# First four up-projection tiles taken from x times the second norm's gain, with the norm's factor and the shift applied to the result; ffn state and first up weights loaded behind the head loop

## What is computed

```
x = x + gate1 * mixed                       # mixed = concat(...) @ w_o, [520, 1024]
h2 = rms_norm(x, norm2_g) * (1.0 + scale2) + shift2
up, ffn_buf_new = causal_dwconv(h2 @ w_up, ffn_buf, ffn_conv_w, ffn_conv_b)   # 2 * 2816 columns
val, gt = jnp.split(up, 2, axis=-1)
x = x + gate2 * ((jax.nn.gelu(gt) * val) @ w_down)
```

## Time and profile before

| | us |
|---|---|
| median of 3 runs (lowest to highest) | 948.32 (946.69 to 949.16) |
| the profiled execution | 949.23 |
| its span, first to last instruction | 947.4 |
| granted TensorE clock, mean | 0.991 of full |

### The profile page before, as it was taken

One profiled execution on the slowest core, in us unless ns is written; L12 is line 12 of the kernel. 1 busy time (PEld: TensorE's weight loads), 2 busy tenths in 40 slices (PEclk: granted clock), 3 DMA queues, 4 the chain that ended last, 5 costly groups with the idle time before them and its releaser, 6 DMA issues.

```text
span 947.4 us, 20112 instructions
## 1 busy us (share of the span) xinstructions
PE 919.8 (97%) x7805; PEld 858.7 (91%) x7805; DVE 637.4 (67%) x1241; ACT 513.1 (54%) x1147; POOL 184.3 (19%) x163
## 2 busy tenths in 40 slices
PE   5899999999999999999999989999999999999998
PEld 3588876799999999999899979999999999999997
DVE  2893378488888888888863667777777777722321
ACT  2414845689889889898863354444444443311111
POOL 0032323333333324333330301100000001000000
PEclk9999999999999999999998999999999999999999
DMA  9996732300212203202130423333333331653202
GB/s 338 332 281 222 223 134 102 146 2 23 91 59 77 90 24 112 90 24 90 46 91 23 113 60 90 89 89 90 92 96 98 97 97 50 161 153 80 63 1 91
DMA packets 107897, 100.12 MB, mean 106 GB/s; under 512 B 7125, under 2 KB 96597, under 8 KB 105770
## 3 DMA queue, kind: packets, MB, share of 16 engines
q1 hardware_dynamic: 104030, 77.91, 28.1%
q0 software_dynamic: 3456, 20.97, 6.2%
q10 hardware_dynamic: 340, 0.27, 0.1%
HBM read 96.41 MB, written 2.94 MB: 105 GB/s over the span
## 4 chain that ended last, share of the span: by engine, by line
PE 88%; DVE 6%; ACT 2%; DMA 2%; issue 1%; SPq 0%; POOL 0%; DVEq 0%; ACTq 0%; POOLq 0%
PE ps L890 51%; PE ps L1286 20%; PE ps L885 6%; PE ps L1247 2%; PE ps L1183 2%; PE ps L923 2%; DMA RW<-w_ada 2%; PE ps L1062 1%; PE ps L896 1%; PE ps L1282 1%; DVE RB L1996 1%; PE ps L1209 1%; DVE input_low L1929 1%; DVE up_weights_low L2371 0%; DVE small L1970 0%
## 5 line engine op out<-in xcount | busy, mean ns | idle before, releaser
L890 PE MATMUL ps<-normed_high,up_weights_high 128*128 128x260 f32 x704 | 142.5, 284 | 2.5 <-DVE normed_low L2392 2.4
L890 PE MATMUL ps<-normed_high,up_weights_low 128*128 128x260 f32 x704 | 142.5, 284 | 0.0
L890 PE MATMUL ps<-normed_low,up_weights_high 128*128 128x260 f32 x704 | 142.1, 284 | 0.0
L1791 ACT ACTIVATE up_weights_high<-RW 128x1024 fp32r<-128x1024 f32 x44 | 46.6, 1061 | 128.0 <-PE ps L890 128.0
L836 POOL TENSOR_TENSOR latents_low<-RB,latents_high 128x512 fp32r<-128x512 f32 x64 | 82.7, 1292 | 165.7 <-ACT latents_high L1667 165.6
L1286 PE MATMUL ps<-key_weights_high,latents_high 128*128 128x260 f32 x512 | 113.3, 302 | 0.1
L890 PEld LDWEIGHTS ps<-normed_high,up_weights_high 128*128 128x128 f32 x704 | 108.9, 189 | 3.1 <-issue 2.2
L890 PEld LDWEIGHTS ps<-normed_high,up_weights_low 128*128 128x128 f32 x704 | 109.1, 189 | 0.0
L890 PEld LDWEIGHTS ps<-normed_low,up_weights_high 128*128 128x128 f32 x704 | 108.7, 189 | 0.0
L1286 PE MATMUL ps<-key_weights_high,latents_low 128*128 128x260 f32 x512 | 103.1, 283 | 0.0
L1286 PE MATMUL ps<-key_weights_low,latents_high 128*128 128x260 f32 x512 | 103.1, 283 | 0.0
(11 more groups left out here) (350 smaller groups left out, 2069.5 us busy)
## 6 DMA issues: line engine op xcount, KB each, us to landing
RW<-w_ada SPq DMA_DIRECT2D x24, 1024.0 KB, 7.0
RW<-w_up SPq DMA_DIRECT2D x44, 512.0 KB, 5.1
RW<-w_down SPq DMA_DIRECT2D x8, 1408.0 KB, 7.3
RW<-w_in SPq DMA_DIRECT2D x11, 512.0 KB, 6.4
RB<-w_o SPq DMA_DIRECT2D x8, 512.0 KB, 4.2
RB<-x_prompt SPq DMA_DIRECT2D x2, 1024.0 KB, 12.2
o_y_p<-RB SPq DMA_DIRECT2D x4, 448.0 KB
cst<-consts SPq DMA_DIRECT2D x1, 844.5 KB, 12.0
```

The source lines that it names most:

```text
L890: last = mm(ps[j % 4][rows[0]:rows[1], h, 0:H], lhsT, src[:, h * H:(h + 1) * H], start=start, stop=stop)
L1791: A(wuH[:, KT * g:KT * g + KT, :], wup[:, c, KT * g:KT * g + KT, :], ACT.Copy).then_inc(s_whi, 1)
```

## The change

For the first four up tiles (lap 0) the kernel uses that the factor rstd is one number for each token. It multiplies x by gain = (1 + scale2) x norm2_g only (`x_high`, `x_low`), takes the product with the up weights, multiplies the result by `rs` (`first_scaled`, DVE) and adds the product of the shift as a bias (`first_evacuate`, ACT, and a small addition for the samples). For the shift's product the nine shift columns, and three more to fill, stand behind the 520 tokens: 532 columns, two halves of 266. The normed x (`hH`, `hL`) is still made, for laps 1 to 10, by the same two steps (the samples' columns now within them).

The order of each engine is rewritten around that. SP: state and first up weights are loaded before w_o tile 5. PE: the state's turns before output tile 6; no fillers; the norm's two sums inside the first up tile. ACT: Square and gained copy of x before `out_high`; up weights at k = 2; the state's copy at k = 5. DVE: gain and shift parts before the residuals; gained low parts and the samples' steps within them; the up weights' low parts at m = 3; then first_scaled 0, low part 3, the rest of `scaled`, first_scaled 1, and the eight `normed_low` between the second low part and the GELU wait of `mlp(0, 0)`. Slots: state and norm sum move to slot 3, the up tiles start in slot 1.

Cut to its core (addresses, semaphore names and the renumbering of jobs are left out):

```diff
@@ SP @@
             for m in range(KT):
+                if m == 5:
+                    bfull(sp, "pv", NS)
+                    sp.dma_start(fs_tok, t["state_ffn_conv"].rearrange("l b r (m c) -> (l r m) b c", c=P)).then_inc(s_fst, 16)
+                    for c in range(2):
+                        up_weights(c, bass.ds(P * c, P))
...
-            for m in range(2):
-                up_weights(m, bass.ds(P * m, P))
-            full(sp, J_WO[KT - 1])
-            sp.dma_start(fs_tok, t["state_ffn_conv"].rearrange("l b r (m c) -> (l r m) b c", c=P)).then_inc(s_fst, 16)
@@ PE @@
             for m in range(4, KT):
+                if m == 6:
+                    claim(pe, J_FST)
+                    pe.wait_ge(s_fst, 16)
+                    for b in range(NS):
+                        c = 512 * (b // 4) + 4 * FT * (b % 4)
+                        last = tr(flat(J_FST)[:, c:c + 4 * FT], fs_tok[:, b, :], 4 * FT)
+                    last.then_inc(psum_full[J_FST % 4], 1)
...
+            def first_products(e, g, k):
+
+                j = up_job(2 * e + g)
+                for n, (w, x) in enumerate(((wuH, x_high[k]), (wuH, x_low[k]), (wuL, x_high[k]))):
+                    for h in range(2):
+                        last = mm(ps[j % 4][:, h, 0:XH], w[:, KT * g + k, :], x[:, h * XH:(h + 1) * XH],
+                                  start=(k == 0 and n == 0), stop=(k == KT - 1 and n == 2))
...
+            for e in range(2):
+                for g in range(2):
+                    up_start(e, g, 0)
+                    for k in range(KT):
+                        if (e, g) == (0, 0):
+                            pe.wait_ge(s_xlo, k + 1)
+                            if k in (0, 4, KT - 1):
+                                pe.wait_ge(s_xs, 1 + (0, 4, KT - 1).index(k))
+                        last = first_products(e, g, k)
+                        if (e, g) == (1, 1) and k < KT - 1:
+                            last.then_inc(s_xused, 1)
+                        if (e, g, k) == (0, 0, 1):
+                            claim(pe, J_N2)
+                            pe.wait_ge(s_nsum, KT - 2)
+                            both(J_N2, ones, sq[:, 0, :], True, False)
+                        if (e, g, k) == (0, 0, 3):
+                            pe.wait_ge(s_sq, 2 * KT + 12)
+                            both(J_N2, ones, sq[:, KT - 1, :], False, True).then_inc(psum_full[J_N2 % 4], 1)
@@ ACT @@
             for k in range(KT):
+                act.wait_ge(s_x1, k + 1)
+                A(sq[:, k, :], xT[:, k, :], ACT.Square).then_inc(s_sq, 1)
+                A(x_high[k][:, 0:NP], xT[:, k, 0:NP], ACT.Identity, bias=small[:, 1:2], scale=gmod[:, k, 0:1]).then_inc(s_xhi, 1)
                 if k + 4 < KT:
                     out_high(k + 4)
-                act.wait_ge(s_x1, k + 1)
-                A(sq[:, k, :], xT[:, k, :], ACT.Square).then_inc(s_sq, 1)
-                if k == 3:
+                if k == 2:
                     bfull(act, "pv", NS)
                     up_high(0, 0, 1)
                     up_high(0, 1, 1)
...
+            def first_evacuate(n):
+
+                j = up_job(n)
+                act.wait_ge(s_first, n + 1)
+                A(UU[n // 2][:, n % 2, 2:2 + NP], scaled_up[:, 0:NP], ACT.Identity, bias=shifts_up[n % 2][:, 0:1]).then_inc(psum_free[j % 4], 1)
...
             up_high(1, 0, 1, up_job(0))
...
+            first_evacuate(0)
+            up_high(1, 1, 1, up_job(1))
+            first_evacuate(1)
+            up_high(0, 0, 2, up_job(2))
+            for k in range(KT):
+                normed_high(k)
+            first_evacuate(2)
+            act.wait_ge(s_cv, 1)
+            A(GE, CV[1], ACT.Gelu_apprx_tanh).then_inc(s_ge, 1)
+            up_high(0, 1, 2, up_job(3))
+            first_evacuate(3)
@@ DVE @@
             for m in range(KT):
                 residual(J_WO[m], m, 2 * KT, s_x1, m + 1)
                 if m + 4 < KT:
                     out_low(m + 4)
-                if m == 4:
+                if 0 < m < KT - 1:
+                    gained_low(m - 1)
+                if m == 3:
                     up_low(0, 0, 1)
                     up_low(0, 1, 2)
...
+                if m == 4:
+                    gained_samples(0, 4)
+                if m == 6:
+                    gained_samples(4, KT - 1)
+                    gained_low(KT - 2)
+            gained_samples(KT - 1, KT)
+            gained_low(KT - 1)
...
+            def scaled(k):
+
+                V.tensor_tensor(h2[:, k, NP:T], gsr[:, k, :], dshift[:, k, :], ADD)
+                V.scalar_tensor_tensor(h2[:, k, 0:NP], xT[:, k, 0:NP], gmod[:, k, 0:1], rs[:, 0:NP], MUL, MUL).then_inc(s_hp, 1)
...
+            def first_scaled(n):
+
+                j = up_job(n)
+                full(dve, j)
+                if n > 0:
+                    dve.wait_ge(psum_free[up_job(n - 1) % 4], free_value(up_job(n - 1)))
+                shift = shifts_up[n % 2]
+                st.did(V.tensor_copy(shift, ps[j % 4][:, 1, T - XH:T + 9 - XH]))
+                st.did(V.tensor_tensor(scaled_up[:, 0:XH], ps[j % 4][:, 0, 0:XH], rs[:, 0:XH], MUL))
+                st.seq(V.tensor_tensor(scaled_up[:, XH:T], ps[j % 4][:, 1, 0:T - XH], rs[:, XH:T], MUL))
+                V.tensor_tensor(UU[n // 2][:, n % 2, 2 + NP:2 + T], scaled_up[:, NP:T], shift[:, 1:9], ADD).then_inc(s_first, 1)
+
+            dve.wait_ge(s_rs, 7)
+            st.seq(V.tensor_tensor(gsr[:, :, :], gs[:, :, :], rs[:, NP:T].unsqueeze(1).to_broadcast([P, KT, NS]), MUL))
+            scaled(0)
+            scaled(1)
+            first_scaled(0)
+            up_low(1, 0, 3)
+            for k in range(2, KT):
+                scaled(k)
...
+            first_scaled(1)
+            mlp(0, 0, 2, normed_lows)
+            first_scaled(3)
+            mlp(0, 1, 2)
+            with dve.Fori(1, FT // 2 - 1) as i:
```

189 lines of the change are left out of this document (97 added, 92 removed).

## The result

| | before | after |
|---|---|---|
| median (lowest to highest), us | 948.32 (946.13 to 949.97), 20 runs | 950.24 (947.12 to 953.99), 20 runs |
| ratio after / before, 95% interval | | 1.0024 (1.0014 to 1.0034) |
| profiled execution, us | 949.23 | 948.87 |
| its span | 947.4 | 947.1 |
| granted clock, mean | 0.991 | 0.995 |

A forecast was written before the change was run, and what follows sets the result against it. PE bounds the kernel, with a 10.7 us hole waiting for the norm before the up projection. Items of 11.05 replace it (+0.3); clock 1.2 and POOL contention 1.0 make +2.5, so 950.8 us, range 945.0 to 955.5.

The forecast's parts named there:

- the clock term: After the sixth up tile's wait PE may restart at half clock: 1.2 us net, bounds 0 and 3.4.
- Items 1 and 3: Output projection: tile 4 waits 0.75 us for its low weights, tile 7 waits 1.1 for tile 4's slot.
- Item 2: The state's eight turns move into the output projection: 0.85 us, and 0.14 until slot 3 is evacuated.
- Item 4: The norm's two sums move inside the first up tile: 2.0 us, and 0.1 waiting for the last POOL addition.
- Contention: DVE and POOL operations slow each other where they fall together at 542 to 549: 1.0 us, bounds 0 and 2.5.
- Item 6: The sixth up tile waits 5.2 us for its low part: DVE's queue of 31.5 against PE's 26.4.
- Item 7: The seventh up tile waits 0.4 us: DVE's convolution and low part take 6.15 against PE's 5.77.
- Rival A: The forecast itself: the hole is traded for a wait at the sixth up tile; 947 to 952.5 us, chance 0.47.
- Rival B: Faster: DVE reaches the sixth low part in time by overlap or earlier GELU; 944.0 us, chance 0.16.
- Rival C: Slower: DVE and POOL exclude each other from 538 to 549, delaying slot and second sum; 953.8 us, chance 0.30.
- Rival D: First tiles' operands are late too, leaving a 3 to 4 us hole before the up projection; 954.3 us, chance 0.07.
- The hidden terms: Early loads, small gain and shift operations on DVE, and the state's copy on ACT stand in existing waits, costing nothing.

The follow-up runs named there:

- e4: The changed kernel with ACT's out_high(k + 4) ahead of Square and gained copy, and DVE's two first up low parts behind residual 4; 949.80 us, ratio 1.0028.
- e8: The changed kernel with POOL adding only 8 of 520 columns of the squares, so its norm is wrong (a probe); 950.32 us, ratio 1.0029.
- e1: The changed kernel with the first GELU issued ahead of first_evacuate(2) on ACT; 947.44 us, ratio 0.9998.
- e10: The changed kernel with the third up tile's low part made twice on DVE; 950.50 us, one run.
- e2: The changed kernel with ten filler matmuls between the fifth up tile and the wait for the sixth low part; 950.97 us, ratio 1.0040.
- e5: The changed kernel with the sixth up low part right behind normed_low, and ACT's sixth high part and GELU before the third tile's evacuation; 948.69 us, ratio 1.0011.
- e6: e5 with the seventh, eighth and ninth up low parts also moved earlier on DVE, ACT's high parts in the same order; 943.17 us, ratio 0.9948.
- e7: e6 with e4's two edits, and the norm's sums behind the fifth and seventh step of the first up tile; 941.74 us, ratio 0.9939.
- e3: The kernel before with only the early state and up-weight loads, turns before output tile 6, state's copy on ACT and after's slots; 949.29 us, ratio 1.0007.
- e9: e7 with the tenth and eleventh up low parts also moved earlier on DVE, ACT's high parts likewise; 942.23 us, ratio 0.9943, on another chip.
- e11: e6 with the third up tile's low part made twice on DVE; 946.45 us, one run.
- e12: The changed kernel again without any edit, on another chip; 951.28 us, ratio 1.0031.

## Why the prediction was right, point by point

The forecast of 950.8 was 0.6 over the median; D came out at +2.53 for +2.5. That is closer than its terms deserve. As prices its terms add up to 13.2 in place of the hole's 10.7, and D gives 13.2 too (10.7 + 2.53), but counted from start to start single terms are off by up to 0.3 either way, and the clock term agreed by luck.

- **Items 1 and 3, the stops at output tiles 4 and 7.** Forecast 0.75 and 1.1, seen 0.78 and 1.06 of idle time, released as foretold by the low weights and by residual 4's second half. Counted from the start of one product to the start of the next they cost 1.0 and 1.3, as the idle time counts from a modelled end. Their mechanism was right, but they could not be won back singly: e4 took both away, half of the gain went into a longer wait at the sum and the rest, and more, into the half clock behind that wait. The hole taken as a sum of PE's stops was right as bookkeeping and wrong as a list of what each stop is worth.
- **Item 2, the turns.** Forecast 0.85, seen 0.6 (531.23 to 531.81); the slot's 0.14 did not show.
- **Item 4, the sums inside the first tile.** I gave each pair 1.0 and the wait 0.1. The pairs took 0.76 and 0.68 (547.26 to the product of 548.02, 549.70 to 550.38), the wait 0.86. The sentence that PE would pass the first tile without a stop was wrong in this step: I had looked at the low parts of x and at the last Square, and left out that DVE's rows ahead of it would be stretched (1.1 at 539.92, 0.26 at 544.27), which I had priced only as a lump in another place. DVE came to residual 7 at 547.59, which is 550.5 on the scale of before (the first residual stands 2.92 later there), where I had 548.9.
- **Contention, 1.0 (bounds 0 and 2.5).** Measured by e8: 1.13 at the sixth tile, with the additions' own length in it. The wait of 0.86 is its visible part, so item 4 and contention together were forecast at 3.1 and came to 2.3 (0.86, 0.76 and 0.68), or 2.8 with the slower first products behind each.
- **Item 5, 266 columns.** Forecast 0.5, measured 0.75: three such tiles take 17.87 (552.81 to 570.68), 5.96 each for 5.77. The forecast scaled 5.765 by the columns alone.
- **Item 6, the sixth tile.** Forecast 5.2, measured 5.18. The queue from rstd to the sixth low part's end was 30.1, where I had 29.9. Inside it two errors cancel: the four first_scaled took 3.9 for 4.4, the wait for GELU 2.8 for 2.6 and the hidden tile 2.1 for 1.85. e1 and e10 confirm the mechanism from both sides: 2.8 less and 1.25 more on that queue moved the wait by 2.89 and 1.27.
- **Item 7, the seventh tile, and the clock.** No wait there in after, since the slow clock hid it, and 1.3 for the clock; in e2, where the clock stayed at full, 0.48. Forecast 0.4 and 1.2 net. Half a clock for 3 us was the right size for after, but e8, e4, e5 and e10 show 3.9, 5.4, 6.1 and 4.8 us behind waits of 5.2, 5.2, 2.8 and 6.4, so this term was taken right by luck: its bounds 0 and 3.4 were the honest statement. The forecast had no term for a second fall of the clock; in after there was none, in e4 it cost 1.5.
- **What the sum lacked.** PE's first records behind each stop are slower, 0.1 to 0.2 each time, some 0.8 in all.
- **The table load.** Forecast by the earlier trace rows as 1.28 without a drain; again GELU starts 0.01 behind the load (576.02 + 1.28, GELU at 577.31). The 1380 ns of drain that the Trainium skill (ScalarE: Activation LUTs, What ACT_TABLE_LOAD costs) adds would, by estimate, have made the wait 6.6; it was 5.18.

Rival A stood. Rival B's size was right for another kernel: I put the win of a DVE in time at 6.8, and e6 gives 6.77, but by due times and not by overlap. Of rival C the mechanism is real, at 1.1 and not 3; e4 shows that it can reach 2.2 of DVE time when the order is unlucky, though e7 pays the same 2.2 and is 1.8 faster than e6. Rival D did not occur. The hidden terms held, as far as e3 shows: the early loads and the moved copy together at nothing. What stays open is why the clock stays low for 3 us after one wait and for 6 after another that is shorter.

## What to carry to other kernels

When a change takes work off the critical engine, list the queue of the helper engine from the event that releases it to the next thing that the critical engine needs, and compare the two lengths: here, by the forecast, 31.5 against 26.4 us, and the 5 us between them, with the clock behind, ate the whole gain. Then order the helper's queue by due time, with what has no buffer behind it first; the same instructions in another order turned +0.24% into -0.5% (e6). A stop of the critical engine is worth its length only if it does not come back as a wait further on, and a longer wait there can bring the half clock with it, as in e4. So test removals together and not one by one, and read the clock behind every wait before you blame the helper.

## What was unexpected in the hardware

- The clock of TensorE went to half in stretches that belong to no change: from about 496 to 504 us in the traces of before, e1, e2, e3, e9, e11 and e12, not in those of after, e4 to e8 and e10. The first residual starts at 516.9 to 518.4 with it and at 513.7 to 516.1 without. A shorter one, from about 166 to 170, stands in before, e1, e6, e7 and e11, and with it e6 and e7 have the two latest starts of those without the first. They are the largest part of the run-to-run spread that I can point to.
- After waits of 2.3, 2.8, 5.2 and 6.4 us in the up projection the clock was at half for 3.2, 6.1, 3.0 to 5.4 and 4.8 us of PE's work, so between 1.3 and 2.6 us lost, with no order by the wait's length. By the granted clock alone the half stretches near 582 are 3.4 us long in after, e1 and e12 and 6.8 in e4, e5, e8 and e10; what differs besides is how much of them falls into the wait. In these the clock fell while PE still waited, in e8 3 us ahead of the end (PE idle from 575.3, half from 577.5, products again from 580.4). Behind the waits of 2.0, 2.1 and 3.2 us around the norm in e4, before and e3 it fell 1.4, 1.8 and 1.1 us after PE had resumed.
- After waits of 0.8 to 1.1 us (output tiles 4 and 7, the first sum in after) the clock stayed at full.
- A DVE copy of 32 columns can take 1.30 us when it meets a POOL addition of 520, and the POOL addition can take 2.21 for 1.31: each is held until the other has ended.
